# A decoder step on one core: the sample tile first and on column groups, gate products ahead of the last turns, the router with its weights stationary

## What is computed

```python
q, k, v, qi, ki, wi, u, vb, ga, gb = project_inputs(x, pos, w_in, gate_bias)   # ga, gb after a sigmoid
# gMLP, prompt: chunks of 128 positions, 4 channel groups
vn  = layer_norm(vb, ln_v_g, ln_v_b)
mix = einsum('gts,bcsgd->bctgd', tril(w_spatial), vn) + b_spatial
gm  = u * mix
# gMLP, sample: only position 0 of its chunk: mix = w_spatial[:, 0, 0] * vn + b_spatial[:, 0]; vn is an output
merged = ga * (attn_out @ w_branch_a) + gb * (gm @ w_branch_b)
h = layer_norm(DEEPNORM_ALPHA * x + merged @ w_o, ln1_g, ln1_b)
# hierarchical MoE: 4 group logits and 32 expert logits per token
lg = h @ w_router_group + b_router_group;  le = h @ w_router_expert + b_router_expert
```

## Time and profile before

| | us |
|---|---|
| median of 3 runs | 1595.13 (1594.96 to 1598.93) |
| the profiled execution, its own time | 1585.32 |
| its span, first to last instruction | 1583.8 |
| TensorE busy | 1440.6 (91%) |
| VectorE busy | 733.8 (46%) |
| ScalarE busy | 283.7 (18%) |
| GpSimd busy | 254.5 (16%) |
| TensorE's mean granted clock | 0.951 of full speed |

### The profile page before, as it was taken

How to read it: one execution, slowest core, us unless ns; L and a number is a source line. 1 busy time by engine, 2 the same in 40 slices (tenths; PEclk the granted TensorE clock), 3 DMA queues, 4 the chain that set the end, 5 groups by cost and what they waited for, 6 DMA issues and landing times. The chain is left out here.

```text
span 1583.8 us, 17679 instructions
## 1 busy us (share of the span) xinstructions
PE 1440.6 (91%) x5634; PEld 778.2 (49%) x5634; DVE 733.8 (46%) x1662; ACT 283.7 (18%) x620; POOL 254.5 (16%) x308
## 2 busy tenths in 40 slices
PE   7999999799979999998998898999299999999944
PEld 2444444344346666665776564555244444444410
DVE  0101023788888889932659445555311111111127
ACT  0100122112121111111564200000011111111112
POOL 3131000033310000101351000111111111111103
PEclk9999999799989999999999999999599999999967
DMA  9221001400021112201331394000189898989639
GB/s 313 63 64 33 15 15 67 126 0 1 0 96 69 60 60 86 76 28 38 98 109 57 114 355 195 27 27 27 45 339 351 339 349 337 354 334 348 249 92 249
DMA packets 74504, 221.88 MB, mean 140 GB/s; under 512 B 16738, under 2 KB 42338, under 8 KB 65098
## 3 DMA queue, kind: packets, MB, share of 16 engines
q1 hardware_dynamic: 58170, 184.64, 33.3%
q0 software_dynamic: 14992, 35.90, 6.4%
q10 hardware_dynamic: 1280, 0.53, 0.2%
HBM read 190.56 MB, written 38.84 MB: 145 GB/s over the span
## 5 line engine op out<-in xcount | busy, mean ns | idle before, releaser
L1713 PE MATMUL main_ps_experts<-w_gate_up,main_e_rowsT 128*128 128x512 f32 x512 | 227.7, 598 | 1.2 <-DVE main_e_rowsT L1812 1.2
L234 PE MATMUL ps_front<-front,x_all 128*128 128x512 f32 (+1 forms) x448 | 183.8, 566 | 1.7 <-ACT wi L364 1.7
L854 DVE TENSOR_SCALAR_CACHE_REDUCE front<-score,bound 128x384 bf16<-128x384 f32 (+2 forms) x198 | 174.2, 942 | 19.2 <-DVE bound L880 18.9
L1713 PEld LDWEIGHTS main_ps_experts<-w_gate_up,main_e_rowsT 128*128 128x128 f32 x512 | 95.7, 192 | 110.6 <-issue 110.6
L234 PEld LDWEIGHTS ps_front<-front,x_all 128*128 128x128 f32 x448 | 84.5, 193 | 93.8 <-issue 83.3
L1465 PE MATMUL ps_merge<-w_o,mergedT 128*128 128x512 f32 x256 | 118.4, 623 | 3.0 <-DVE h_rows L1586 3.0
L1817 DVE TENSOR_TENSOR main_hidden<-main_hidden,main_ps_experts 128x256 f32<-128x256 f32 x32 | 13.5, 421 | 221.1 <-ACT main_hidden L1766 221.1
L1740 PE MATMUL main_ps_experts<-w_down,main_hiddenT 128*128 128x512 f32 x256 | 115.3, 593 | 0.5 <-ACT main_hiddenT L1771 0.5
L712 PE MATMUL ps_gate<-x_all,w_gate 128*128 128x344 f32 x384 | 114.9, 458 | 0.3 <-ACT front L788 0.3
L712 PE MATMUL ps_gate<-x_all,front 128*128 128x344 f32 x384 | 113.2, 453 | 0.0
L712 PEld LDWEIGHTS ps_gate<-x_all,w_gate 128*128 128x128 f32 x384 | 73.5, 192 | 38.7 <-issue 1.2
(11 more groups left out here) (277 smaller groups left out, 1753.7 us busy)
## 6 DMA issues: line engine op xcount, KB each, us to landing
w_gate_up<-in_w_gate_up SPq DMA_DIRECT2D x32, 2048.0 KB, 9.1
w_down<-in_w_down SPq DMA_DIRECT2D x32, 1024.0 KB, 12.1
w_gate_up<-pair_out SPq DMA_DIRECT2D x16, 512.0 KB, 18.3
front<-in_w_qkvi SPq DMA_DIRECT2D x8, 930.0 KB, 12.7
w_gate<-in_w_gate SPq DMA_DIRECT2D x4, 1280.0 KB, 6.3
front<-in_w_gate SPq DMA_DIRECT2D x4, 1280.0 KB, 6.1
h_rows<-in_x_rows SPq DMA_DIRECT2D x9, 512.0 KB, 6.0
h<-h_rows SPq DMA_DIRECT2D x9, 512.0 KB, 2.6
```

The source lines that it names most:

```text
L234: mm = nc.tensor.matmul(ps[:, g % 2, 0:c1 - c0], x_all[:, k, t * P:(t + 1) * P], w[:, k, c0:c1], start=(k == 0), stop=(k == KC - 1))
L854: V.tensor_scalar(waste[0:n, at - width:at], s, column(bound, g), None, compare, ALU.add, accum_out=column(number, g)).then_inc(taken, 1)
L1713: mm = nc.tensor.matmul(ps[:, GU, :], rowsT[j][:, k, :], w_gu[jw][:, k, :], start=(k == 0), stop=(k == KC - 1))
```

## The change

In `choose_keys_and_gate`:

- The sample tile is made first (`make_few`): its 1024 columns of u and v are cut into four quarters of 256, each multiplied on its own column group of TensorE (PSUM partitions 0, 32, 64 and 96 on) into one bank. ScalarE copies the quarters to partitions 0 to 7 and sums them (`read_few`). It no longer waits for the constants at the stage's start but at the first bias step. Tile numbers i now run from 0 (sample) to 8; SyncE stores the sample's v rows after tile 0, and ScalarE waits for that store before it writes the same buffer again.
- The turn of tile 7, the mix and the turn of tile 8 move into the first `make_gates`: the first two before the third product of unit 0, the last before unit 1.
- The place transposes (`turn_places`) move from before unit 18 to behind unit 19, and the row searches of the sample queries to behind units 20 to 23, two each.
- The staggered loops of ScalarE and GpSimd are written out.

In `merge_and_route`: the router's weights become the stationary operand, so that the logits come out as 36 rows of 128 tokens. ScalarE copies them to SBUF (`lgT`), TensorE turns them back (`turn_logits`), and VectorE reads those. Within a step the order becomes `project(i)`, `route(i-1)`, `rank(i-2)`, `turn_logits(i-1)`.

```diff
@@ -591,6 +591,8 @@
         rows_f = sb("rows_f", [P, 2 * N_SAMPLE])
         ps = ctx.enter_context(nc.psum_tensor("ps_gate", [P, 8, 512], F32))
         U, V, MIX, TURN = 0, 1, 2, 3
+        FEW_BANK, FEW_SQUARES, FEW, QUARTER = 4, 5, 32, GW // 2
+        LAST = TILES - 1
         SETS = ((4, 5, 6), (7, 0, 1))
...
@@ -632,9 +635,9 @@
                 sp.dma_start(to, src.to_broadcast([P, src.shape[1]]) if src.shape[0] == 1 else src).then_inc(const_in, 16)
 
             sp.dma_start(w_gate[0], ins["w_gate"][0]).then_inc(w_gate_in[0], 16)
-            sp.wait_ge(normed, TILES)
-            sp.dma_start(outs["chunk_v"], vb[(TILES - 1) % 2][0:N_SAMPLE, :]).then_inc(chunk_out, 16)
-            sp.wait_ge(uv_full, TILES * 2)
+            sp.wait_ge(normed, 1)
+            sp.dma_start(outs["chunk_v"], vb[0][0:N_SAMPLE, :]).then_inc(chunk_out, 16)
+            sp.wait_ge(uv_full, 1 + NT * 2)
             sp.dma_start(w_gate[1], ins["w_gate"][1]).then_inc(w_gate_in[1], 16)
             sp.dma_start(keep["v"][:], outs["v_all"][0:SEQ, :].rearrange("(t p) n -> p t n", p=P)).then_inc(v_in, 16)
...
@@ -661,50 +664,68 @@
 
         @block.tensor
         def _(pe):
-            def make_uv(t, j):
-                n = N_SAMPLE if isinstance(t, int) and t == TILES - 1 else P
+            def make_few():
+                for k in range(KC):
+                    if k >= KC // 2:
+                        pe.wait_ge(w_uv_in[k], 16)
+                    for g in range(4):
+                        mm = nc.tensor.matmul(ps[g * FEW:g * FEW + N_SAMPLE, FEW_BANK, 0:QUARTER], x_all[:, k, SEQ:SEQ + N_SAMPLE],
+                                              w_uv(k)[:, g * QUARTER:(g + 1) * QUARTER], start=(k == 0), stop=(k == KC - 1))
+                mm.then_inc(uv_full, 1)
+
+            def make_uv(t):
                 for b in (U, V):
-                    pe.wait_ge(uv_read, t * 2 + b + 1)
+                    if t >= 1:
+                        pe.wait_ge(uv_read, 2 * t - 1 + b)
                     for k in range(KC):
-                        if isinstance(t, int) and t == 0 and b == U and k >= KC // 2:
-                            pe.wait_ge(w_uv_in[k], 16)
-                        mm = nc.tensor.matmul(ps[0:n, b, :], x_all[:, k, bass.ds(t * P, n)], w_uv(k)[:, b * GW:(b + 1) * GW],
+                        mm = nc.tensor.matmul(ps[:, b, :], x_all[:, k, t * P:(t + 1) * P], w_uv(k)[:, b * GW:(b + 1) * GW],
                                               start=(k == 0), stop=(k == KC - 1))
                     mm.then_inc(uv_full, 1)
 
...
-            staggered(pe, TILES, [(0, make_uv), (1, mix), (2, turn)], loop=False)
-            pe.wait_ge(gm_read, TILES + 1)
-
-            def make_gates(i, between=None):
+            make_few()
+            for i in range(1, TILES):
+                make_uv(i - 1)
+                if i >= 2:
+                    mix(i - 1)
+                    turn(i - 2)
+
+            def last_mix(at, which):
+                if (at, which) == (0, 2):
+                    turn(LAST - 1)
+                    mix(LAST)
+                if (at, which) == (1, 0):
+                    turn(LAST)
+                    pe.wait_ge(uv_read, 2 * NT)
+                if (at, which) == (2, 2):
+                    pe.wait_ge(gm_read, TILES)
+
+            def make_gates(i, ahead=None, between=None):
                 for j in range(2):
                     pe.wait_ge(w_gate_in[j], i * 16 + 16)
                     for p, (c0, n) in enumerate(PIECES):
                         at = j * 3 + p
                         for which in range(3):
...
-            make_gates(0)
+            make_gates(0, ahead=last_mix)
             with pe.Fori(1, KC // 2 - 1) as i:
                 make_gates(i)
 
-            pe.wait_ge(placed, 1)
...
+            def turn_places():
+                pe.wait_ge(placed, 1)
+                for g in range(PAGES):
+                    nc.tensor.transpose(ps[:, MIX, g * N_SAMPLE:(g + 1) * N_SAMPLE], score_s[:, g * P:(g + 1) * P],
+                                        ident[0:N_SAMPLE, 0:N_SAMPLE])
+                nc.tensor.transpose(ps[0:1, MIX, 256:256 + N_SAMPLE], score_s[:, PAST:PAST + 1],
+                                    ident[0:N_SAMPLE, 0:N_SAMPLE]).then_inc(place_turned, 1)
 
             def find_rows(at):
-
-                for b in ((0, 1), (2,), (3,), (4, 5), (6,), (7,))[at]:
+                if at == 1:
+                    turn_places()
+                for b in ((), (), (0, 1), (2, 3), (4, 5), (6, 7))[at]:
                     pe.wait_ge(hot_ready, b + 1)
...
@@ -742,53 +765,73 @@
 
         @block.scalar
         def _(act):
-            act.sem_inc(uv_read, 2)
-            act.sem_inc(gm_read, 1)
             act.sem_inc(gates_read, 6)
-            act.wait_ge(const_in, 16 * N_CONST)
-
-            def read_uv(t, j):
-                act.wait_ge(uv_full, t * 2 + 1)
-
-                if not (isinstance(t, int) and t < 2):
-                    act.wait_ge(gm_turned, t - 1)
+
+            def read_few():
+                act.wait_ge(uv_full, 1)
+                for g, to in enumerate((u[0], u[0], vb[0], vb[0])):
+                    c = slice(g % 2 * QUARTER, (g % 2 + 1) * QUARTER)
+                    nc.scalar.copy(to[0:N_SAMPLE, c], ps[g * FEW:g * FEW + N_SAMPLE, FEW_BANK, 0:QUARTER]).then_inc(few_step, 1)
+                squares, stats, v = ps[0:N_SAMPLE, FEW_SQUARES, :], stat[0][0:N_SAMPLE, :], vb[0][0:N_SAMPLE, :]
+                act.wait_ge(few_step, 4)
+                nc.scalar.activation(squares, v, ACT.Copy, accum_out=stats[:, 0:1]).then_inc(few_step, 1)
+                act.wait_ge(few_step, 5)
+                nc.scalar.mul(stats[:, 1:2], stats[:, 0:1], -1.0 / GW).then_inc(few_step, 1)
+                act.wait_ge(few_step, 6)
+                nc.scalar.activation(squares, v, ACT.Square, bias=stats[:, 1:2], accum_out=stats[:, 2:3]).then_inc(few_step, 1)
+                act.wait_ge(few_step, 7)
+                nc.scalar.mul(stats[:, 2:3], stats[:, 2:3], 1.0 / GW).then_inc(few_step, 1)
+
+            def read_uv(i):
...
+                act.wait_ge(uv_full, 2 * t + 2)
+                if i >= 2:
+                    act.wait_ge(gm_turned, i - 1)
                 nc.scalar.copy(u[j][:], ps[:, U, :]).then_inc(uv_read, 1)
-                act.wait_ge(uv_full, t * 2 + 2)
+                act.wait_ge(uv_full, 2 * t + 3)
+                if i == 2:
+                    act.wait_ge(chunk_out, 16)
...
+                act.wait_ge(uv_read, t * 2 + 2)
                 nc.scalar.mul(stat[j][:, 2:3], stat[j][:, 2:3], 1.0 / GW).then_inc(act_step, 1)
...
-            staggered(act, TILES, [(0, read_uv), (1, read_mix), (2, read_turned)])
+            read_few()
+            for i in range(1, TILES + 2):
+                if i < TILES:
+                    read_uv(i)
+                if i <= TILES:
+                    read_mix(i - 1)
+                if i >= 2:
+                    read_turned(i - 2)
             with act.Fori(0, KC // 2) as i:
                 for j in range(2):
                     for p, (c0, n) in enumerate(PIECES):
...
-            def normalise(t, j):
-                step = Chain(pool, pool_step, t * 4)
-                wait_alone(pool, act_step, t * 3 + 3, idle[2])
...
+            def normalise(i):
+                n, j = P if i else N_SAMPLE, i % 2
+                stats, v = stat[j][0:n, :], vb[j][0:n, :]
+                step = Chain(pool, pool_step, i * 4)
+                if i == 0:
+                    pool.wait_ge(few_step, 8)
+                else:
+                    pool.wait_ge(act_step, i * 3)
+                step(nc.gpsimd.tensor_scalar(stats[:, 3:4], stats[:, 2:3], EPS, None, ALU.add))
...
+            for i in range(TILES):
+                normalise(i)
+                if i >= 1:
+                    gate_u(i - 1)
+            gate_u(LAST)
...
@@ -1334,6 +1386,7 @@
         off_group = sb("off_group", [P, N_GROUPS])
         marked, rest, waste = (over[:, D + n * N_EXPERTS:D + (n + 1) * N_EXPERTS] for n in range(3))
         highest = sb("highest", [P, 1])
+        lgT = over[0:ROUTER, D + 3 * N_EXPERTS:D + 3 * N_EXPERTS + P]
...
@@ -1480,8 +1534,12 @@
                 if i >= 1:
                     pe.wait_ge(logits_read, i)
                 for k in range(KC):
-                    mm = nc.tensor.matmul(ps[:, 2, 0:ROUTER], hT[:, k, :], w_r[:, k, :], start=(k == 0), stop=(k == KC - 1))
+                    mm = nc.tensor.matmul(ps[0:ROUTER, 2, 0:P], w_r[:, k, :], hT[:, k, :], start=(k == 0), stop=(k == KC - 1))
                 mm.then_inc(routed, 1)
+
+            def turn_logits(i):
+                pe.wait_ge(lgT_read, i + 1)
+                nc.tensor.transpose(ps[:, 2, P:P + ROUTER], lgT, ident[0:ROUTER, 0:ROUTER]).then_inc(lg_turned, 1)
...
@@ -1499,10 +1557,12 @@
                     project_few()
                 elif i < TILES:
                     project(i)
+                if 1 <= i <= TILES:
+                    route(i - 1)
```

(10 more changed lines are left out.)

83 lines of the change are left out of this document (39 added, 44 removed).

## The result

The changed kernel took **1571.5 us** (median of 4 runs, 1570.2 to 1576.0), the kernel before beside it 1595.4 us (4 runs). The ratio is 0.985, with a 95% interval of 0.983 to 0.988: 23.9 us faster. The forecast was 30.8 us and 1564.3, with a range up to 1571.5; the measured time lies at that upper edge.

The account below looks back on a forecast made before the run. TensorE, busy 91% of the span, was taken as the bound, racing VectorE's search in the gate stage. Terms -23.2 + 2.1 - 5.1 - 4.6 = -30.8 from 1595.1 gave 1564.3 us; 8-in-10 range 1559 to 1571.5.

Parts of the forecast that it names:

- sample tile: Start of the gate stage: the sample tile on four column groups takes 6.1 us, saving TensorE 10.3 us.
- second unit earlier in the stage: Gate products: the second unit begins at 440.9 us instead of 464.45, 23.5 us earlier.
- end of the search, into the stage: VectorE's key-bound search in the gate stage: untouched by the change, so it still ends at 662.0 us.
- gate stage: Two units of gate products move ahead of the search's end, gaining 2 x 11.6 = 23.2 us.
- router, per tile: Stationary router weights with copy and turn of logits: net +0.3 us a tile, seven of these +2.1 us.
- slow projections: Merge stage: three of seven projections behind a route, 1.7 us too long each, become normal: -5.1 us.
- end of the router: Last tile's route no longer stands behind a rank waiting for VectorE's picking: -4.6 us.
- A: Clock keeps falling in the router: 1569.4 us with three slow projections, 1576.2 with all seven; chance 0.28.
- B: The sample tile's column groups don't run side by side: 16.4 us for its passes, total 1573.3 us; chance 0.05.
- D: Slower than before: clock stays at 1.2 GHz in the u/v stage after the sample tile, 1604 us; chance 0.03.
- part 3: Place transposes behind two more gate-product units, row searches in the last four: gain 23.2 us, set by the search.
- Rival C: The search ends later through GpSimd's gate multiplies, by up to 2.5 us: 1566.8 us; chance 0.06.

Follow-up runs that it names:

- the repeats: The kernel before and the changed kernel, each unchanged, executed again on one chip: 1581.7 and 1563.3 us, gate stage 450.2 and 432.3 us.
- all three kernels: Kernel before, changed kernel, and changed kernel with GpSimd's large gate-stage operations cut to one column: search 366.4, 369.6 and 357.7 us.
- the filler: Changed kernel plus 14 TensorE passes with unread results ahead of the place transposes: gate stage 428.1 us.
- the plain sample tile: Changed kernel with the sample tile still first but made as 32 plain passes, without column groups: gate stage 432.9 us.
- the two without gate products: Changed kernel and kernel before, each with GpSimd's 24 gate multiplies left out: search 365.5 and 363.7 us.

## Why the prediction was off

By its own steps, with the sum's terms:

| term | forecast | measured | from |
|---|---|---|---|
| sample tile | 6.1 us | 6.04 | after, 292.12 to 298.16 |
| wait at the last turn | 0.5 | 0.26 | after, 436.65 |
| second unit earlier in the stage | 23.5 | 23.8 | 168.8 - 145.0 |
| TensorE at the search, into the stage | 365.1 | 365.0 | after, 661.74 - 4.67 - 292.12 |
| end of the search, into the stage | 366.4 | **369.6** | after, line 955 |
| time behind the search | 58.7 | **62.0 to 62.4**, by the low clock | 81.9 - 23.2 = 58.7 |
| gate stage | -23.2 | **-16.7** | 448.3 to 431.6 |
| router, per tile | +0.3 | +0.42 | 18.21 - 17.79 |
| slow projections | -5.1 | -5.0 | 3 x (15.68 - 14.00) |
| end of the router | -4.6 | -5.1; -4.7 in the repeats | below |

The end of the router is the time from the start of the last projection to the last reading of logits: 1124.53 - 1089.01 = 35.5 us before, of which 1.7 were the slow projection, and 1112.41 - 1083.65 = 28.8 after; in the repeats 35.5 and 29.2.

**What was right.** All that TensorE does up to the search, to 0.3 us, and the router: -7.6 us forecast, -7.2 by the rows (7 x 0.42 - 5.0 - 5.1), -6.5 between the repeats. The stage's profiled difference, -5.5, has the first projection in it, whose length varies from 14.00 to 15.70 us with the old router and to 16.95 with the new, and was 15.45 before and 16.95 after. Rivals A, B and D are out: no slow projection behind a route, column groups side by side, the clock up behind the sample tile.

**The step that failed** is part 3, "VectorE isn't touched and ends at 662.0. TensorE waits 1.3 us instead of 0.8". The mechanism was right, that the gain is set by the search and not by TensorE; the end of the search was held fixed, and it isn't. It came 369.6 us into the stage, not 366.4. Rival C priced its delay at up to 2.5 us, by whole multiplies of GpSimd, gave it 0.06, and looked in the wrong place: the additional delay lies in the u/v stage, where the change shifts the tiles of GpSimd against the rounds of VectorE. The trace of before held the warning, a step of 0.23 us that took 1.19. VectorE's timeline of before, and GpSimd's:

```profile
331.52 1.19 DVE L875 SCALAR_TENSOR_TENSOR found_bits<-reached,bit,found_bits 128x7 int32<-128x7 int32 x1
```

```profile
331.42 1.27 POOL L823 TENSOR_TENSOR vb<-vb,ln_v 128x512 f32<-128x512 f32 x1
```

I had read the search's end, and not the spread of its small steps.

The second mistake is in the same sentence. A wait was costed at its length, as if the cover of 1.3 us were all that could be lost. The 3.2 us of delay made a wait of 4.67 us, and behind it the clock was low: another 3.3 us in the profiled execution, 3.7 in the repeat. The rows of before had such a case as well (the stand of 8.62 us and 11.09 for the next pair), and I used it for what the change removes, not for what it might create. Together 3.2 + 3.3 = 6.5 us are all that the gate stage lacks (23.2 - 16.7); the router lacks another 0.4 to 1.1. That the medians lack 6.9 fits, but so closely only by luck, since the stages that nobody changed vary by more. The last step of the sum, that the profiled execution stands 9.8 us under the median in both kernels, failed too: after's stands 0.8 above it, with its long attention stage.

The Trainium skill has the rule for the first mistake, in "SBUF — State Buffer", Who interferes with whom: VectorE and GpSimd share a pair of ports under an exclusive lock, an instruction of VectorE with two SBUF inputs contends with one of GpSimd that reads SBUF, and the one that comes second blocks until the first is done. The trace agrees: 1.19 us instead of 0.23 for line 927, ending with GpSimd's. The same section leaves the form of `tensor_scalar` that also writes its accumulator out of the one-input instructions that can contend; the counting instructions of line 906 agree, with 77.0 us in all three kernels.

## What to carry to other kernels

Two engines that meet at a level point need not be independent: before a gain is bounded by the other engine's end, read how that end may move when the work beside it shifts, from the spread of its shortest instructions, not from their mean. A wait of TensorE can cost its length and then the clock behind it (at the place transposes here: at 2.68 and 4.67 us, not at 0.64 to 0.80), so it pays to place an instruction that waits for another engine a little later than TensorE could take it; moving nine transposes by two products was worth 8 us here, half as much as the whole gate part of the change. And a large saving in TensorE's work ahead of such a point can be worth almost nothing (here some 10 us of passes for 1 us) until the wait is moved.

## What the runs showed of the hardware

- VectorE's instructions of 7 elements that fall on a large GpSimd instruction mostly end with it: they last up to 1.2 us instead of 0.17 to 0.23, also a `TENSOR_SCALAR` with one tensor input (0.94). Of 27 that began during one in the two profiled executions, 25 did, and the two others fell on the `TENSOR_SCALAR` of line 821. Over the search GpSimd cost VectorE 8.7 to 11.9 us of 370.
- Products of 36 moving columns with 128-column loads left three of seven projections slow; with 128 moving columns and 36-column loads, a copy and a turn none was, though the 16 passes take the same time (1.98 and 1.94 us).
- The attention stage has two lengths, 149 to 153 and 163 to 166 us. In the long one a copy by VectorE stands still while GpSimd issues its gathers back to back, three or four times for 14 to 20 us together. VectorE's and GpSimd's timelines of after:

```profile
812.14 0.08 DVE L1313 DVE_READ_ACCUMULATOR2_ANT low<- 128x1 f32 x1
817.78 0.49 DVE L1225 COPY probsT<-ps_attn 128x128 f32<-128x128 f32 x2 [5.56 <-DMA x_all<-in_x_tiles]
```

```profile
811.65 0.95 POOL L1073 DMA_INDIRECT v_sel<-in_cache_v,rows  x1 [0.30 <-DVE low L1313]
812.91 0.93 POOL L1078 DMA_INDIRECT k_sel<-out_k_all,own_row  x1 [0.30 <-issue]
814.15 0.96 POOL L1073 DMA_INDIRECT v_sel<-in_cache_v,rows  x1 [0.30 <-issue]
815.41 0.95 POOL L1073 DMA_INDIRECT v_sel<-in_cache_v,rows  x1 [0.30 <-issue]
```

The release that the view names, a transfer of the first stage, can't be the cause; that the gathers are is argued from their place, not shown, and why one execution has the stall and another not stays open. The four kernels that ran together on one chip (the filler, the plain sample tile, and the two without gate products) all had the long stage, the kernel before among them, so it is no effect of the change; the four of each of the two other chips all had the short one. So the chip, or the moment, is a rival to how the instructions fall, and no run tells them apart. No run spaced the gathers out.
